# Inverting the 128x128 unit-triangular matrices of the gated delta rule: 16x16 diagonal blocks by rows on VectorE, the upper three levels on TensorE

## The reference, cut to what matters

```
lmat = jnp.where(strict, beta[..., :, None] * kk * decay, 0.0)
amat = jnp.eye(CHUNK) + lmat
rhs  = jnp.concatenate([v * beta[..., None], k * (beta * jnp.exp(G))[..., None]], -1)
sol  = lax.linalg.triangular_solve(amat, rhs, left_side=True, lower=True, unit_diagonal=True)
```

## Time and profile before

| | us |
|---|---|
| three runs | 2264.84, 2263.67, 2260.33 |
| median | 2263.67 |
| span of the profiled execution | 2261.5 |
| the profiled execution's own time beside its span | not given; the median of the runs is 2.2 above the span |
| stage with the heads, in the trace | 121 to 709, that is 588 |

### The profile page before, as it was taken

How to read it: one execution, slowest core, us unless ns; L and a number is a source line. 1 busy time by engine, 2 the same in 40 slices (tenths; PEclk the granted TensorE clock), 3 DMA queues, 4 the chain that set the end, 5 groups by cost and what they waited for, 6 DMA issues and landing times.

```text
span 2261.5 us, 24322 instructions
## 1 busy us (share of the span) xinstructions
PE 2066.9 (91%) x10160; PEld 1516.4 (67%) x10160; DVE 943.3 (42%) x1370; ACT 643.6 (28%) x966; POOL 451.9 (20%) x310
## 2 busy tenths in 40 slices
PE   7999999999999979888788879898888899999999
PEld 5878888888887763333333337677655677888787
DVE  7865445433333662111011025865643894222333
ACT  4533422322323311000000024353134763222231
POOL 5432132231322511111111011321001220000021
PEclk9999999999999979998899889999998999999999
DMA  5751421221324369999999964202111133332210
GB/s 168 255 141 47 93 57 38 38 75 45 68 38 152 140 230 397 409 405 406 408 414 406 420 270 169 100 13 72 47 47 37 47 121 122 102 112 75 95 73 38
DMA packets 97657, 361.28 MB, mean 160 GB/s; under 512 B 9850, under 2 KB 34588, under 8 KB 85256
## 3 DMA queue, kind: packets, MB, share of 16 engines
q1 hardware_dynamic: 86800, 335.34, 41.4%
q0 software_dynamic: 8240, 19.00, 2.5%
q10 hardware_dynamic: 2504, 5.35, 0.8%
HBM read 338.94 MB, written 29.10 MB: 163 GB/s over the span
## 4 chain that ended last, share of the span: by engine, by line
PE 81%; DVE 8%; issue 5%; ACT 4%; POOL 1%; DMA 0%; PEld 0%; PEldq 0%; SPq 0%; ACTq 0%; DVEq 0%; POOLq 0%
PE ps L269 77%; PE ps L273 4%; ACT ST L265 1%; DVE H L259 1%; ACT L265 1%; DVE ST L253 1%; DVE BG L253 1%; ACT M L265 1%; DVE sm L2930 0%; DVE WL L253 0%; DVE ML L253 0%; POOL WL L253 0%; ACT M L266 0%; DVE H L256 0%; DVE BG L259 0%
## 5 line engine op out<-in xcount | busy, mean ns | idle before, releaser
L269 PE MATMUL ps<-W,BG 128*64 128x512 f32 x672 | 202.1, 644 | 31.9 <-issue 31.9
L269 PE MATMUL ps<-XH,WS 128*128 128x512 f32 x704 | 218.6, 392 | 0.0
L269 PE MATMUL ps<-HTH,WL 128*128 128x512 f32 x448 | 180.9, 404 | 0.0
L269 PEld LDWEIGHTS ps<-ST 128*128 128x128 f32 x1376 | 167.5, 192 | 8.6 <-POOL ST L253 1.7
L269 PE MATMUL ps<-ST 128*128 128x64 f32 (+1 forms) x1376 | 167.8, 273 | 1.2 <-POOL ST L253 1.0
L269 PEld LDWEIGHTS ps<-XH,WS 128*128 128x128 f32 x704 | 133.4, 189 | 27.8
L2100 DVE COPY BG<-ps 128x512 f32<-128x512 f32 x32 | 22.1, 692 | 293.0 <-PE ps L269 293.0
L269 PEld LDWEIGHTS ps<-W,BG 128*64 128x64 f32 x672 | 62.1, 148 | 120.0 <-issue 118.5
L269 PE MATMUL ps<-XL,WS 128*128 128x512 f32 x352 | 138.1, 392 | 1.8 <-DVE XL L253 1.8
L269 PE MATMUL ps<-M,BG 128*64 128x512 f32 (+1 forms) x336 | 122.7, 552 | 15.7 <-issue 8.4
L263 ACT ACTIVATE BG<-ps 128x512 f32<-128x512 f32 x48 | 28.5, 595 | 377.8 <-PE ps L273 344.2
(11 more groups left out here) (384 smaller groups left out, 4343.2 us busy)
## 6 DMA issues: line engine op xcount, KB each, us to landing
W<-in_w SPq DMA_DIRECT2D x42, 2048.0 KB, 26.3
W<-in_w_in SPq DMA_DIRECT2D x27, 2048.0 KB, 10.3
ST<-in_w SPq DMA_DIRECT2D x14, 2048.0 KB, 25.4
U<-in_w SPq DMA_DIRECT2D x14, 2048.0 KB, 28.0
M<-in_w SPq DMA_DIRECT2D x13, 2048.0 KB, 28.3
HT<-in_w SPq DMA_DIRECT2D x13, 2048.0 KB, 27.9
W<-in_w_ffn_in SPq DMA_DIRECT2D x22, 1024.0 KB, 7.6
ypad<-BG SPq DMA_DIRECT2D x23, 512.0 KB, 15.1
```

Source lines behind the costliest of these rows:

```text
L269: return p.e.matmul(o, lhsT=l, rhs=r, start=start, stop=stop, skip_group_check=True)
```

## The change

Levels 1, 2, 4 and 8 of the doubling go. In their place the 16x16 diagonal blocks are inverted directly on DVE:

- POOL masks C = (same 16x16 block) * LT, and clears two shared buffers for each pair.
- `v_sub_take`: a TENSOR_REDUCE folds the 8 blocks of each chunk into 16 columns; four chunks and two heads give 8 lanes of the shared buffer LANES.
- `v_sub_turn`: a 32x32-blockwise transpose brings it to rows of blocks.
- `v_sub_rows`: rows 1 to 15 of all blocks of both heads, each a TENSOR_TENSOR of 2*i*i elements and a TENSOR_REDUCE over it that wait for each other; they are spread over four rounds.
- `v_sub_back` transposes back, `v_sub_spread` writes XT of each head.

The buffers are shared by the pair (X and Y of both sets), so this runs once for each pair, in the odd head's steps, and the even head waits for it too. PE has five empty head steps there. Then PE does three levels (16, 32, 64). At each, y and xt are formed as before; xx is gone, and in its place PE transposes the corrected XT (`p_turn4`, a round of its own) and ACT copies the halves that are needed to X. A pair takes 29 rounds, the stage 116. The dense program is as long as before, so its last step lies in round s0b of the last pair, and six working rounds have none. Semaphores: `gm_w_s` shares the masks', the store of the residual shares its load's, the rope table shares the meta tokens'.

```diff
-LEVELS = [1, 2, 4, 8, 16, 32, 64]
+LEVELS = [16, 32, 64]
+DB = 16
...
+        def v_sub_take(h):
+            LT, C, X, XT, Y, AT = sets[h % 2]
+            v.wait_ge(sub_room, 2 * (h // 2) + 1)
+            v.wait_ge(sub_masked, h + 1)
+            v.e.tensor_reduce(lanes_of(lanes, h), C.rearrange("p c (m i) -> p c i m", i=DB), AX.X, ADD).then_inc(sub_done)
+
+        def v_sub_turn(h):
+            v.wait_ge(sub_done, taken(h))
+            v.e.transpose(ROWS_L, LANES).then_inc(v.up())
+
+        def v_sub_rows(h, i0, i1):
+            v.wait_ge(sub_room, 2 * (h // 2) + 2)
+            for i in range(i0, i1):
+                o = inv[:, i, :, 0:i]
+                v.wait_ge(*v.now)
...
+                z = PROD[:, 0:2 * i * i].rearrange("p (b f j) -> p b f j", b=2, f=i)
+                tt(v, z, inv[:, 0:i, :, 0:i].rearrange("p j b f -> p b f j"),
+                   rows_l[:, i, :, 0:i].unsqueeze(2).to_broadcast([P, 2, i, i]), MUL).then_inc(v.up())
+                v.wait_ge(*v.now)
+                v.e.tensor_reduce(o, z, AX.X, ADD, negate=True).then_inc(v.up())
...
+        def v_sub_spread(h):
+            LT, C, X, XT, Y, AT = sets[h % 2]
+            v.wait_ge(sub_done, 3 * (h // 2) + 3)
+            v.e.memset(seconds(Y, 0), 0.0).then_inc(v.up())
...
             p_spread(("eg", h), b0 + 2, h, eGr)
             yield
+            for _ in range(5):
+                yield
             p.wait_ge(xt0_done, h + 1)
             p_turn4(("x0", h), b0 + 1, XT)
             yield
             p.wait_ge(*B["x0", h].free())
-            for n in range(1, 7):
...
+            for n in range(3):
...
-                if n < 6:
-                    p_half(("xx", h, n), b0 + 1, XT, firsts(Y, n))
                 p_half(("xt", h, n), b0 + 2, Y, seconds(XT, n))
                 yield
+                if n < 2:
+                    p.wait_ge(*B["xt", h, n].free())
+                    p_turn4(("xx", h, n), b0 + 1, XT)
+                    yield
...
-            tt(v, C, over4(lv[:, 0:P]), LT, MUL).then_inc(v.up())
-            v.wait_ge(*v.now)
-            tt(v, XT, over4(ident), C, SUB).then_inc(xt0_done)
...
+            v_sub_take(h)
+            yield
+            if h % 2:
+                v_sub_turn(h)
+                v_sub_rows(h, 1, 7)
+            yield
+            if h % 2:
+                v_sub_rows(h, 7, 11)
+            yield
+            if h % 2:
+                v_sub_rows(h, 11, 14)
+            yield
+            if h % 2:
+                v_sub_rows(h, 14, DB)
+                v_sub_back()
+            yield
+            v_sub_spread(h)
```

More of the change, by code:

```diff
@@ L947, in build @@
         lc_done = [sem(f"level{j}") for j in range(2)]
+        sub_room, sub_masked, sub_done = sem("sub_lanes_and_unit"), sem("sub_masked"), sem("sub_taken_or_solved")
         hsq_done = sem("o_squares")
+        LANES, ROWS_L, INV, PROD, COLS_X = (x.rearrange("p c t -> p (c t)") for x in (
+            sets[0][2], sets[1][2], sets[0][4], sets[1][4], sets[1][2]))
+        lanes, cols_x = (x.rearrange("p (i x) -> p i x", x=32) for x in (LANES, COLS_X))
+        rows_l, inv = (x.rearrange("p (i b f) -> p i b f", b=2, f=DB) for x in (ROWS_L, INV))
@@ new lines, in build, with lanes_of, taken @@
+        sub_mask = lv[:, 0:P]
+        def lanes_of(x, h):
+            return x[:, :, 4 * (h % 2):4 * (h % 2) + 4].rearrange("p i x -> p x i")
+        def taken(h):
+            return 3 * (h // 2) + h % 2 + 1
+        def v_sub_take(h):
[3 more added lines that the diff above has]
+            v.e.tensor_reduce(lanes_of(lanes, h), C.rearrange("p c (m i) -> p c i m", i=DB), AX.X, ADD).then_inc(sub_done)
@@ new lines, in v_sub_back @@
+        def v_sub_back():
+            v.wait_ge(*v.now)
+            v.e.transpose(COLS_X, INV).then_inc(sub_done)
+        def v_sub_spread(h):
+            LT, C, X, XT, Y, AT = sets[h % 2]
+            v.wait_ge(sub_done, 3 * (h // 2) + 3)
+            v.e.memset(seconds(Y, 0), 0.0).then_inc(v.up())
+            tt(v, XT.rearrange("p c (m i) -> p c m i", i=DB),
+               sub_mask.rearrange("p (m i) -> p m i", i=DB).unsqueeze(1).to_broadcast([P, 4, P // DB, DB]),
+               lanes_of(cols_x, h).unsqueeze(2).to_broadcast([P, 4, P // DB, DB]), MUL).then_inc(xt0_done)
@@ L1031, in p_head @@
             p.wait_ge(*B["kt", h].free())
-            p.wait_ge(*B["xt", h, 6].free())
+            p.wait_ge(*B["xt", h, 2].free())
             p_products(("w", h), b0 + 2, lambda c: KG[:, c, :], lambda c: XT[:, c, :])
@@ L1133, in v_head @@
             tt(v, q4, q4, four(t.at), MUL).then_inc(t.drained)
-            v.wait_ge(*B["kk", h].free())
-            v.wait_ge(*B["at", h].free())
-            tt(v, C, over4(lv[:, 0:P]), LT, MUL).then_inc(v.up())
-            v.wait_ge(*v.now)
-            tt(v, XT, over4(ident), C, SUB).then_inc(xt0_done)
+            v_sub_take(h)
[15 more added lines that the diff above has]
+            v_sub_spread(h)
             yield
             yield
-            for n in range(1, 7):
+            for n in range(3):
                 yield
[L1143 to L1150, removed]
                 t = B["xt", h, n]
@@ L1167, in v_head @@
             v.wait_ge(*t.full())
-            v.wait_ge(*B["xx", h, 5].free())
+            v.wait_ge(*B["y", h, 2].full())
             tt(v, VB, four(t.at), col4(beta[:, :, h]), MUL).then_inc(t.drained)
@@ L1192, in s_head @@
             act(C, four(t.at), ACT.Exp).then_inc(t.drained)
-            yield
-            yield
-            yield
+            for _ in range(8):
+                yield
             t = B["x0", h]
             s.wait_ge(*t.full())
-            act(X, four(t.at), ACT.Copy).then_inc(t.drained)
+            act(firsts(X, 0), firsts(four(t.at), 0), ACT.Copy).then_inc(t.drained)
             yield
-            for n in range(1, 7):
+            for n in range(3):
                 t = B["y", h, n]
@@ L1205, in s_head @@
                 yield
+                if n < 2:
+                    t = B["xx", h, n]
+                    s.wait_ge(*t.full())
+                    act(firsts(X, n + 1), firsts(four(t.at), n + 1), ACT.Copy).then_inc(t.drained)
+                    yield
             yield
@@ L1236, in g_head @@
             tt(g, C, C, col4(rk[:, :, h]), MUL).then_inc(D_done)
[L1237 to L1242, removed]
+            if h % 2 == 0:
+                g.e.memset(LANES, 0.0).then_inc(sub_room)
+            yield
+            g.wait_ge(first_done, 2)
+            g.wait_ge(kd_done, h + 1)
+            g.wait_ge(*B["kk", h].free())
+            g.wait_ge(*B["at", h].free())
+            tt(g, C, over4(sub_mask), LT, MUL).then_inc(sub_masked)
+            if h % 2 == 0:
+                g.e.memset(INV, 0.0).then_inc(g.up())
+                g.wait_ge(*g.now)
+                g.e.memset(INV[:, 0:496:33], 1.0).then_inc(g.up())
+                g.e.memset(INV[:, 16:512:33], 1.0).then_inc(sub_room)
+            yield
+            for n in range(3):
+                if n == 0:
+                    g.wait_ge(sub_done, taken(h))
                 else:
                     g.wait_ge(*B["y", h, n - 1].full())
-                tt(g, C, over4(lv[:, n * P:n * P + P]), LT, MUL).then_inc(lc_done[h % 2])
+                tt(g, C, over4(lv[:, (n + 1) * P:(n + 2) * P]), LT, MUL).then_inc(lc_done[h % 2])
+                for _ in range(8 if n == 0 else 3):
+                    yield
+            for _ in range(11):
                 yield
[L1247 to L1253, removed]
+        c_h0, c_h0s, v_gelu, gw_done = sem("residual_loaded_or_stored"), sem("h0_stored"), sem("gm_v"), sem("gm_ws_turned")
+        c_gw = c_lv
         h0v = h0d.rearrange("(i p) d -> p i d", p=P)
```

43 lines of the change are left out of this document (23 added, 20 removed).

## The result

The changed kernel takes 2212.78 us (median of 4 runs, 2205.35 to 2214.61) where the kernel before took 2262.03 (4 runs): ratio 0.978, interval 0.976 to 0.980, 49 us less. The forecast was 2224, range 2196 to 2256.

A forecast was written before the change was run, and what follows sets the result against it. PE's own instructions were taken to bound the stage. The terms -69.3 - 4.9 + 22.3 + 6.8 + 3 + 2 = -40.1 us, taken from 2263.7, gave 2224 us, range 2196 to 2256.

The forecast's parts named there:

- PE's work, -69.3: On PE in the stage: 704 half-product records go (76.0 us), 64 transposes come (6.7 us); 69.3 us less.
- Waits ahead of x0, -4.9: PE's present waits for DVE's XT ahead of the turn x0 go, 4.9 us less.
- DVE late, +22.3: New PE waits before x0 or a dense step: DVE late by 10.9, 6.8, 3.5 and 1.1 us by pair.
- The chain, 18.4 in 16.1 to 20.7: DVE's new work per pair between the first head's eg and x0: 18.4 us, the middle of 16.1 to 20.7.
- its 1.5 a pair: DVE time lost beside POOL's work, 1.5 us a pair.
- The rival that charged every strided element: DVE's chain costs 20.7 us a pair and POOL takes 2.4; total 2247 us, chance 0.18 for 2236 to 2252.
- The clock, +6.8: PE's granted clock drops after a stall once a pair, some 1.7 us lost each, 6.8 us together.
- Shorter level rounds, +3: Rounds with a turn are shorter on PE and cover less; 1 us in three rounds, 3 us (0 to 8).
- The tail, +2: Last pair's rounds s1a to s3b, without dense steps: PE waits for ACT or DVE, 2 us (1 to 4).
- The sum: All terms of the stage together, -40.1 us, taken from the span of 2261.5 and the median of 2263.7.

The follow-up runs named there:

- experiment 8: The kernel before with all seven levels kept and only the third product replaced by a turn of XT in its own round; 2302.73 us, ratio 1.0178.

## Why the prediction was right, and where its terms were off

- **PE's work, -69.3.** The counts came as said (x384, x96). The size was some 5 us too small: in the kernel without rows, whose loss to the clock is the same as before (17.0), PE is busy 500.0 us where it was 575.0, 75.0 less. The traces of the two show where. Adding up, over the stage, the distance from each row of PE to the next, less idle time, the 64-column products went from 118.5 to 40.8 us (-77.7, forecast -76.0), the turns from 18.8 to 25.4 (+6.6, forecast +6.7), all else but dense matmuls rose by 0.9, and the dense matmuls, of which there are as many, went from 349.8 to 345.2. The forecast had nothing for them. A part of it is visible in the kernel before: the first dense matmul behind a block of the heads' products costs more than the next ones.

```profile
307.28 1.89 PE L269 MATMUL ps<-ST 128*128 128x64 f32 x16
308.98 0.48 PE L269 MATMUL ps<-WL,HTH 128*128 128x512 f32 x1
...
309.52 0.40 PE L269 MATMUL ps<-WV,HTL 128*128 128x512 f32 x1
```

  From 308.98 to the next start, 309.30, it is 0.32, from there to 309.52 it is 0.22. The kernel without rows has 84 such places instead of 103: 1.7 us at 0.09 each. The other 3 us of the dense matmuls aren't explained.
- **Waits ahead of x0, -4.9, and DVE late, +22.3.** In the trace x0 waits 11.3, DVE's low parts 4.9, the sums 4.9: 21.1. Without the rows 21.4 us of idle time go. The total was right, and in part by luck, since its parts were less so: 13.7, 0.4, 3.8 and 3.2 us by pair where 10.9, 6.8, 3.5 and 1.1 were forecast. The first pair was undersized: beside POOL a convolution took 3.91 us of tensor work instead of 2.33, another (169.12, behind x0 and ahead of the sums) 4.28, and a low part 3.12 instead of 1.21, together 5.4 us where the prediction allowed 1.5. The second pair got off with 0.4 since PE stood for POOL at d32 meanwhile, which the prediction didn't have.
- **The chain, 18.4 in 16.1 to 20.7.** From start to next start, as the prediction counts, the rows took 12.2, 13.9, 14.9 and 16.4 us by pair, where it had 10.9. In the first pair no row instruction met POOL's work; there the eg rows, takes, transposes, clearing and spread add 5.8, and the chain is 18.0, near the forecast. What the other pairs have more is lost beside POOL: one or two row instructions in each took 1.2 to 2.3 us, like the one at 302.60. The prediction had such losses in its 1.5 a pair; in every pair they were more. Strided access costs: a product (0.93 - 0.15)/450 = 1.73 ns an element against (0.63 - 0.15)/450 = 1.07 with adjacent words; the take (1.04 - 0.15)/512 = 1.74. In cycles of 1.04 ns that is 0.6 to 0.7 more, in the middle of the 0 to 1.1 that the prediction left open. The Trainium skill ("Vector Engine (DVE) Microarchitecture Reference", section 5.2) gives 1.7 to 2.5 ns where a port finds no two adjacent words in a row, against 1.05: the measurement stands at its lower end. The row reductions read flat and cost (0.62 - 0.15)/450 = 1.04; the prediction had rightly left them out of its strided elements. The rival that charged every strided element put 1.1 cycles on each, too much.
- **The clock, +6.8.** The loss went up by 5.1 and 8.6 in the two profiles; without the rows it is back at 17.0. But that sum counts idle stretches too. PE's busy time, where a lower clock shows as cost, is 1.5 and 6.0 us above the kernel without rows, so 6.8 was too high, by little or by much.
- **Shorter level rounds, +3.** The place was wrong, the kind right. Beside the wait for the sums at 173.64, counted above, and the 2.7 us for a dense copy that was there before, the level rounds show almost no wait. The 3.5 us (4.81 less 1.31) lie in the empty rounds, at d32.
- **The tail, +2.** This term failed: it is zero. From 647.8 to 654.8, with no dense step, the window is

```profile
647.80:654.80 7.00, 7.00 (x57) 6.40 (x55) 1.39 (x4) 2.54 (x8) 0.00 (x0) 1.00 0.80 291
```

  with PE busy throughout; the rows of the two heads follow each other there, which by my reading is what covers the hand-overs. Behind it stands the same 0.94 us as in the earlier trace rows.
- **The sum.** Stage -54.8 and -50.0 in the profiles against -40.1. Busy time, in which the clock's loss shows too, was forecast at -69.3 + 6.8 = -62.5 and came to -75.0 + 1.5 = -73.5 and -75.0 + 6.0 = -69.0; idle time was forecast at +22.4 and came to +18.6 and +18.9. So most of what the forecast lacked is PE's busy time: 5.7 us of its work, and the clock by 0.8 to 5.3.

Open: 3 us of the dense matmuls; why the times of one kernel spread over 9 us (2205 to 2214) with the same waits (PE's idle time in the stage 33.3 and 33.6), only at another granted clock; how much of each loss behind a stall belongs to that stall; and what the meetings with POOL cost in time, since no run moved POOL's low parts away from the chain.

## What to carry to other kernels

Work moved from the bound engine to an idle one pays by what the bound engine sheds, less what the other is late at the hand-over; read that from the other engine's busy share beside the chain (here 95% in the first pair up to 173.6 us, though 52% over the stage). Where that stretch is full, neither another order nor more steps of the bound engine helped here; leaving the rows out gave 24 us, and 1.3 to 1.7 us less of them a pair nothing that could be measured. And when the work of a bound engine thins out, look for chains over several engines that it used to cover: one such gave a wait (d31 to d32) that no added instruction points to.

## What the runs showed of the hardware that was not expected

A DVE instruction of 8 elements took 2.30 us beside POOL's low part, where the same one takes 0.17 otherwise. DVE's row, and POOL's:

```profile
568.60 2.30 DVE L255 TENSOR_TENSOR ST<-ST 128x8 f32<-128x8 f32 x1
```

```profile
568.50 2.38 POOL L255 TENSOR_TENSOR WL<-W,WHS 128x1024 fp32r<-128x1024 f32 x1
```

They end together: DVE stood until POOL was done. The price doesn't shrink with the instruction: 2.1 us were lost on 8 elements here, 1.7 on the 200 at 302.60. Splitting work into many tiny instructions should make such a meeting likelier, though no run varied that. The other surprise is the clock: in the kernel of experiment 8, fourteen waits of 1.9 to 5.9 us came with a loss of 48.9 us, more than the idle time itself (40.7). After 5.92 us of idle time at 336.85 the four-microsecond windows from 337 to 345 are at 0.50, that is 1.2 GHz, with PE busy all through.
